# Router logits taken from the turned residual rows, with the norm factor, scale and shift applied to small tensors

## The reference

```python
sh1, sc1, g1, sh2, sc2, g2 = modulation(cond, mod_w, mod_b)
x = x + g1 * mixer(rms_norm(x, norm1) * (1 + sc1) + sh1)      # ends in: out = cat @ w_out
x = x + g2 * hierarchical_moe(rms_norm(x, norm2) * (1 + sc2) + sh2)
# in hierarchical_moe, xt = its input rows:
g_logits = xt @ rg_w + rg_b          # 4 groups: the best one
e_logits = xt @ re_w + re_b          # 32 experts: the best two of that group
y = grouped_expert_mlp(xt, expert_idx, weights, e_wg, e_wu, e_wd)
```

## Time and profile before

| | us |
|---|---|
| median of 3 runs | 1406.06 (1405.39 to 1408.11) |
| profiled execution | 1406.54 |
| its span in the trace | 1404.7 |
| busy in the span: PE, DVE, ACT, POOL | 1191.0, 706.3, 280.4, 107.9 |
| HBM traffic | 320.31 MB read, 25.51 MB written |

### The profile page before, as it was taken

How to read it: one execution, slowest core, us unless ns; L and a number is a source line. 1 busy time by engine, 2 the same in 40 slices (tenths; PEclk the granted TensorE clock), 3 DMA queues, 4 the chain that set the end, 5 groups by cost and what they waited for, 6 DMA issues and landing times.

```text
span 1404.7 us, 20219 instructions
## 1 busy us (share of the span) xinstructions
PE 1191.0 (85%) x7522; PEld 668.9 (48%) x7522; DVE 706.3 (50%) x1625; ACT 280.4 (20%) x700; POOL 107.9 (8%) x163
## 2 busy tenths in 40 slices
PE   5999999889787887897869999988979579699781
PEld 3455545654452544554434554556435354356450
DVE  3365877682467132232363687877634733223224
ACT  1211153750112000000032103356211100000000
POOL 2000000001000211111000000000100012012100
PEclk9999999999887898999989999999998779899896
DMA  9321101348149999999961101024561499999996
GB/s 376 150 94 47 54 21 60 129 172 338 77 166 381 407 421 418 419 419 419 397 247 53 71 33 58 1 75 175 220 276 72 180 348 417 419 419 419 419 413 249
DMA packets 59762, 334.58 MB, mean 238 GB/s; under 512 B 10672, under 2 KB 10672, under 8 KB 27404
## 3 DMA queue, kind: packets, MB, share of 16 engines
q1 hardware_dynamic: 45216, 295.78, 52.1%
q0 software_dynamic: 14448, 37.50, 7.1%
HBM read 320.31 MB, written 25.51 MB: 246 GB/s over the span
## 4 chain that ended last, share of the span: by engine, by line
PE 43%; DMA 21%; SPq 14%; DVE 10%; issue 5%; ACT 3%; DVEq 2%; PEld 1%; POOL 1%; PEldq 0%; ACTq 0%; POOLq 0%
PE bank L1762 12%; SPq L389 11%; DMA ring<-in_stream 11%; PE bank L1693 9%; DMA U<-in_stream 5%; PE bank L2061 4%; PE bank L2178 4%; DMA U<-in_n2row 3%; PE bank L2211 3%; SPq L387 2%; DVE U L1276 1%; PE bank L1637 1%; PE bank L1850 1%; DMA U<-moe_out 1%; PE bank L1876 1%
## 5 line engine op out<-in xcount | busy, mean ns | idle before, releaser
L1762 PE MATMUL bank<-HT,ring 128*128 128x512 f32 (+1 forms) x640 | 175.4, 435 | 2.0 <-issue 2.0
L2178 PE MATMUL bank<-ring,HT 128*32 128x256 f32 (+2 forms) x800 | 146.1, 433 | 33.7 <-DMA U<-in_stream 25.0
L2178 PE MATMUL bank<-U,HT 128*32 128x256 f32 (+2 forms) x992 | 151.7, 413 | 20.5 <-DMA ring<-in_stream 9.3
L1693 PE MATMUL bank<-ring,HT 128*128 128x512 f32 x320 | 147.1, 601 | 2.9 <-ACT HT L658 1.5
L1762 PEld LDWEIGHTS bank<-HT,ring 128*128 128x128 f32 x640 | 97.3, 191 | 79.7 <-issue 79.7
L2178 PEld LDWEIGHTS bank<-U,HT 128*32 128x32 f32 (+2 forms) x992 | 87.3, 136 | 59.5 <-issue 39.4
L1119 DVE SCALAR_TENSOR_TENSOR U<-U,prm 128x655 f32<-128x655 f32 x120 | 107.9, 899 | 7.7 <-issue 0.4
L2178 PEld LDWEIGHTS bank<-ring,HT 128*32 128x32 f32 (+2 forms) x800 | 80.2, 143 | 61.7 <-issue 46.3
L2061 PE MATMUL bank<-ring,HT 128*128 128x512 f32 x240 | 106.8, 594 | 0.0
L1555 DVE TENSOR_TENSOR HT<-bank,HT 128x256 f32<-128x256 f32 x32 | 13.6, 424 | 178.8 <-ACT HT L888 178.8
L888 ACT ACTIVATE HT<-bank 128x256 f32<-128x256 f32 x32 | 12.3, 384 | 412.8 <-PE bank L2178 412.8
(11 more groups left out here) (372 smaller groups left out, 1704.5 us busy)
## 6 DMA issues: line engine op xcount, KB each, us to landing
ring<-in_stream SPq DMA_DIRECT2D x142, 1024.0 KB, 14.1
U<-in_stream SPq DMA_DIRECT2D x72, 1024.0 KB, 25.6
spare<-in_stream SPq DMA_DIRECT2D x24, 1024.0 KB, 25.7
RAB<-in_stream SPq DMA_DIRECT2D x14, 1024.0 KB
U<-moe_out SPq DMA_DIRECT2D x20, 512.0 KB, 7.3
U<-in_stream SPq DMA_DIRECT2D x14, 512.0 KB, 20.4
CAT<-in_stream SPq DMA_DIRECT2D x14, 512.0 KB, 22.1
RAB<-mod_rows POOLq DMA_DIRECT2D x12, 512.0 KB, 9.3
```

The costliest lines, as they stand in the source:

```text
L1693: ins = e.matmul(bank[:], HT[:, k, t * P:(t + 1) * P], wide(q, k), start=(k == 0), stop=(k == KD - 1))
L1762: ins = e.matmul(out, wt(q)[:, k, P * (n % 2):P * (n % 2) + P], HT[:, k, lo:lo + w], start=(k == 0), stop=(k == KD - 1))
L2178: ins = e.matmul(PS[2 + p][s, FF * j:FF * j + FF], xgT[:, p, k, s], w, start=(k == 0), stop=(k == KD - 1))
```

## The change

The logits of a row x with norm factor r are r * (x @ (w * rw)) + (shift @ rw + rb), where w = norm weight * (1 + scale). The kernel after computes them in this form. `X` itself is turned (`x_turned`, `x_out` in place of `h2_turned`, `h2_out`), as soon as both halves of its residual are added. The scaled router weights are `rw0` for the context tile and `rw`, scaled in place, for the others. For the scale and shift as columns, PE multiplies the modulation rows in `srow` by two columns of the identity (`columns_of_rows`); the shift's logits are one row per condition (`shift_logits`), which DVE adds to `rb` and PE spreads over the partitions (`spread_shift`). `choice` applies r and adds the spread row, in one instruction per row tile. The normed rows `h2_row` are still made, for the experts. Orders, banks and the split of the choices (three tiles, then two) are changed with it. `residual(9)` stands behind the first choice. POOL waits for the columns before it loads `g1` over `srow`.

```diff
 # POOL, behind rows_out(l, 0, MODC)
+                e.wait_ge(S["shift_ps"], 4 * l + 2)
                 for cc in range(2):
                     e.dma_start(RA[:, cc, :], ...).then_inc(S["ld_g1"], 16)
 # ACT
                 for n in range(2 * NT):
                     if n in (2, 4):
                         cat_out(2 + n // 2)
+                    if 5 <= n < 9:
+                        x_out(n - 5)
                     e.wait_ge(S["x_added"], 10 * l + n + 1)
                     A(sqtmp, ..., ACT.Square, accum_out=small(1600 + n, 1))
...
-                    if n == 5:
-                        h2_out(0)
-                        h2_out(1)
-                for t in range(2, NT):
-                    h2_out(t)
+                x_out(NT - 1)
 # DVE
                 gated_rows(NT - 1, NT)
+                rw = pr("rw", KD, 36)
+                e.wait_ge(S["shift_ps"], 4 * l + 2)
+                e.scalar_tensor_tensor(out=rcol, in0=modcols[1]..., scalar=1.0, in1=pr("n2c")..., op0=ALU.add, op1=ALU.mult)
+                e.tensor_copy(bcol, modcols[0]).then_inc(S["shift_sb"], 1); dr()
+                e.tensor_tensor(rw0, rw, rcol[:, 0, :]..., ALU.mult)
                 cat_out(2)
                 e.wait_ge(S["ld_g1"], 32 * (l + 1))
...
                 residual(0)
                 residual(1)
                 cat_out(3)
+                residual(2)
+                residual(3)
+                cat_out(4)
+                residual(4)
+                e.wait_ge(S["shift_ps"], 4 * l + 3)
+                e.tensor_tensor(crow[0:2, :], crow_ps, pr("rb")[0:2, :], ALU.add).then_inc(S["shift_sb"], 1)
+                e.tensor_tensor(rw, rw, rcol[:, 1, :]..., ALU.mult)
+                residual(5)
+                e.wait_ge(S["shift_ps"], 4 * l + 4)
+                e.tensor_copy(cbias, cbias_ps)
+                e.drain().then_inc(S["shift_sb"], 1)
                 e.wait_ge(S["ld_rows"], 80 * (l + 1))
                 for cc in range(2):
                     e.scalar_tensor_tensor(out=RC[:, cc, :], ...)
-                for t in (0, 2):
-                    residual(2 * t + 2)
-                    residual(2 * t + 3)
-                    if t == 0:
-                        cat_out(4)
-                    y = norm2(t, 2, 1 + t // 2)
-                    h2_row(t, y[:, 0:1])
-                    residual(2 * t + 4)
-                    h2_row(t + 1, y[:, 1:2])
-                    residual(2 * t + 5)
-                h2_row(4, norm2(4, 1, 3))
+                norm2(0, 2, 1)
+                residual(6)
+                h2_row(0)
+                h2_row(1)
+                residual(7)
+                norm2(2, 2, 2)
+                h2_row(2)
+                residual(8)
+                h2_row(3)
...
-                    e.tensor_tensor(lg[:, t], logit_bank(t0)[:, 36 * t0:36 * t1]..., rb, ALU.add)
+                    for u in range(t0, t1):
+                        e.scalar_tensor_tensor(out=lg[:, u], in0=logit_bank(u)[:, 36 * u:36 * u + 36], scalar=small(1500 + u, 1),
+                                               in1=cbias[:, cnd(u), :], op0=ALU.mult, op1=ALU.add)
...
-                choice(0, NT - 1)
+                choice(0, LOGITS)                       # LOGITS = 3
+                residual(9)
+                norm2(4, 1, 3)
+                h2_row(4)
                 e.wait_ge(S["lg_ps"], 2 * l + 2)
-                choice(NT - 1, NT)
+                choice(LOGITS, NT)
 # PE
+                def x_turned(t):
+                    e.wait_ge(S["x_added"], 10 * l + 2 * t + 2)
+                    turned_tile(t, "xT_ps", ("x2T_a",), range(KD), X)
+                def columns_of_rows():
+                    e.wait_ge(S["fill_sb"], mod_chunks(l, 0) + MODC // 2)
+                    e.wait_ge(S["ct_sb_a"], NT * l + 2)
+                    e.wait_ge(S["ct_sb_d"], NT * l + 2)
+                    for i in range(2):
+                        r = slice(32 * i + 32, 32 * i + 34)
+                        for k in range(KD):
+                            ins = e.matmul(modcols[i][:, k, :], srow[r, k * P:(k + 1) * P], ident[r, 32 * i + 32:32 * i + 34], ...)
+                        ins.then_inc(S["shift_ps"], 1)
+                def shift_logits():
+                    for k in range(KD):
+                        ins = e.matmul(crow_ps, bcol[:, k, :], rw[:, k, :], start=(k == 0), stop=(k == KD - 1))
+                    ins.then_inc(S["shift_ps"], 1)
+                def spread_shift():
+                    e.wait_ge(S["shift_sb"], 3 * l + 2)
+                    for c in range(2):
+                        ins = e.matmul(cbias_ps[:, c, :], ident[0:2, c:c + 1].to_broadcast((2, P)), crow[0:2, :], ...)
+                    ins.then_inc(S["shift_ps"], 1)
...
                     projected(2 * t)
-                    cat_turned(t + 2)
+                    if t == 0:
+                        columns_of_rows()
+                    else:
+                        cat_turned(t + 2)
                     projected(2 * t + 1)
                     if t == 0:
-                        e.wait_ge(S["fill_sb"], mod_chunks(l, 0) + MODC // 2)
+                        e.wait_ge(S["shift_sb"], 3 * l + 1)
+                        cat_turned(2)
...
-                h2_turned(0)
+                shift_logits()
+                x_turned(0)
+                spread_shift()
                 projected(6)
-                h2_turned(1)
+                e.wait_ge(S["shift_sb"], 3 * l + 3)
+                x_turned(1)
+                projected(7)
                 logits(0)
+                x_turned(2)
+                projected(8)
                 logits(1)
-                for n in range(7, 10):
-                    projected(n)
-                h2_turned(2)
-                h2_turned(3)
+                x_turned(3)
                 logits(2)
+                projected(9)
                 logits(3)
-                h2_turned(4)
+                x_turned(4)
                 logits(4)
```

More of the change, by code:

```diff
@@ L250, in build @@
         sqtmp = view(INU * SLOT + 3 * D, 512)
+        rw0 = view(INU * SLOT + 3 * D + 512, KD, 36)
+        rcol = view(INU * SLOT + 3 * D + 512 + KD * 36, 2, KD)
+        bcol = view(INU * SLOT + 3 * D + 528 + KD * 36, KD, 2)
+        crow = view(INU * SLOT + 3 * D + 544 + KD * 36, 36)
+        cbias = view(INU * SLOT + 3 * D + 580 + KD * 36, 2, 36)
         colsum = PS[6][:, 0:32]
+        modcols = [PS[2 * i][:, 0:2 * KD].rearrange("p (k c) -> p k c", c=2) for i in range(2)]
+        crow_ps = PS[3][0:2, 64:100]
+        cbias_ps = PS[3][:, 128:200].rearrange("p (c n) -> p c n", c=2)
         frow = RAB[0:2].rearrange("p a b -> p (a b)")[:, D:4 * D]
@@ L2075, in logits @@
                         if k % 4 == 0:
-                            e.wait_ge(S["h2T_a"], 2 * (NT * l + t) + k // 4 + 1)
-                        ins = e.matmul(logit_bank(t)[:, 36 * t:36 * t + 36], HT[:, k, t * P:(t + 1) * P], rw[:, k, :], start=(k == 0), stop=(k == KD - 1))
-                    if t >= NT - 2:
+                            e.wait_ge(S["x2T_a"], 2 * (NT * l + t) + k // 4 + 1)
+                        ins = e.matmul(logit_bank(t)[:, 36 * t:36 * t + 36], HT[:, k, t * P:(t + 1) * P], (rw if t else rw0)[:, k, :],
+                                       start=(k == 0), stop=(k == KD - 1))
+                    if t in (LOGITS - 1, NT - 1):
                         ins.then_inc(S["lg_ps"], 1)
@@ L2098, in _, with before @@
-                h2_turned(2)
-                h2_turned(3)
+                x_turned(3)
                 logits(2)
+                projected(9)
                 logits(3)
-                h2_turned(4)
+                x_turned(4)
                 logits(4)
                 mods, q1 = MODBANK, b + INN + MODC + OUTN
-                e.wait_ge(S["wo_sb"], 10 * (l + 1))
+                ranks = PS[7][:, 0:NE * (NT + 1)].rearrange("p (t n) -> p t n", n=NE)
+                def before(j):
+                    return e.matmul(ranks[:, j + 1:, :], ones16[:].to_broadcast((P, P)), M16[:, j:j + 1, :].to_broadcast((P, NT - j, NE)),
+                                    start=(j == 0), stop=(j == NT - 1), skip_group_check=True)
@@ L2107, in _ @@
                 e.wait_ge(S["lg_sb"], 2 * l + 1)
-                e.matmul(PS[6][:, 0:NE], triS[:], M16[:, 0, :], start=True, stop=True, skip_group_check=True)
-                for j in range(NT - 1):
-                    e.matmul(PS[6][:, NE * (j + 1):NE * (NT + 1)].rearrange("p (t n) -> p t n", n=NE), ones16[:].to_broadcast((P, P)),
-                             M16[:, j:j + 1, :].to_broadcast((P, NT - j, NE)), start=(j == 0), stop=False, skip_group_check=True)
-                e.matmul(PS[6][:, NE:NE * (NT - 1)], triS[:], M16[:, 1:NT - 1, :], start=False, stop=False, skip_group_check=True)
+                e.matmul(ranks[:, 0, :], triS[:], M16[:, 0, :], start=True, stop=True, skip_group_check=True)
@@ L2113, in _ @@
+                for j in range(LOGITS):
+                    before(j)
```

(8 more changed lines are left out.)

47 lines of the change are left out of this document (25 added, 22 removed).

## The result

| | before | after |
|---|---|---|
| median of 4 runs, us | 1406.37 (1405.39 to 1408.11) | 1385.64 (1383.24 to 1387.75) |
| profiled execution, us | 1406.54 | 1387.75 |
| its span, us | 1404.7 | 1386.0 |

The ratio is 0.9851, 95% interval [0.9828, 0.9873]: 20.7 us faster, where I had forecast 12 and a range down to 1386. The unchanged kernel after, run again on another chip, has 0.9848 [0.9821, 0.9875].

A forecast was written before the change was run, and what follows sets the result against it. It took the start of the full expert DMA stream, set by the PE and DVE chain, as the bound. Gains of 7.7 and 9.8 us, less 5.7 for the clock, took 11.8 off 1406.54, forecast 1394 us, range 1386 to 1403.

The forecast's parts named there:

- The bound: Both layers' expert rounds: DMA is full, so each us taken from what starts the stream is one us of time.
- Behind projection 9: Projection 9's end to the choices' end: 13.85 us in place of 19.9, 6.0 us less in each layer.
- PE up to projection 9: Projection 0's start to projection 9's end: PE never stops, 85.9 us; 1.7 and 3.8 us less than before.
- The clock: Light matmuls between projections can drop PE to half clock without idleness; three spells of 1.9 us, 5.7 us in all.
- the eight places: Four light PE places a layer between projections: columns, shift group, logits 0 with a turn, logits 1 and 2 with a turn.
- The rival without any spell: No cold spells on PE: 1406.1 - 17.5 = 1388.6 us; chance 0.22.
- The luck in the sum: Gains of 7.7 us in the first layer and 9.8 in the second, 17.5 us, less 5.7 for the clock: 11.8.
- The stall: PE idle 7.8 or 8.8 us ahead of projection 6 before, plus 3.8 and 4.9 us at half clock; after, none.
- The other engines: Ahead of projection 9: POOL's loads come 2 us later, rows land at about 356 us, with 6 us of cover.
- the margin of DVE: Behind projection 8: DVE has 10.5 us of work against PE's 11.4, about even, DVE just ahead.
- The rival of DVE's order: The first choice starts only when projection 9 ends, giving back 6.5 us a layer; about 1401 us, chance 0.12.
- The slower rival: Added light PE work, dearer columns and a cold spell behind each light place make it slower: 1411.8 us, chance 0.09.

The follow-up runs named there:

- before_split: Kernel before, old arithmetic, with tiles 0 and 1 chosen between residuals 6 and 7 and tiles 2 to 4 at the end; 1416.99 us, ratio 1.0083.
- choice_late: Kernel after with the first choice moved behind residual 9, norm2(4) and h2_row(4), so all choices lie behind projection 9; 1398.23 us, ratio 0.9955.
- cols_x2: Kernel after with each of the 16 column matmuls issued twice, the same values written again; 1399.80 us, ratio 0.9966.
- stall_back: Kernel after, but PE waits ahead of projection 6 until the first normed row tile is made, ahead of residual 6; 1410.57 us, ratio 1.0040.
- before_split2: As before_split on the kernel before, with ranks of tiles 0 and 1 and chunk 0 issued without waiting for the second choice; 1407.24 us, ratio 1.0011.
- rows_early: Kernel after, but DVE waits for the five row loads and builds RC behind cat_out(3), ahead of residual 2; 1391.27 us, ratio 0.9908.
- cols_wide: Kernel after with 32 moving columns in place of 2 in each of the 16 column matmuls; 1384.72 us, ratio 0.9859.
- pool_row4: Kernel after with tile 4's normed row taken off DVE: ACT multiplies by the norm factor, GpSimd does the rest; 1391.48 us, ratio 0.9905.

## Why the prediction was wrong

- **The bound.** Right. The choices' end to the first layer's last scatter took 279.3 to 280.4 us in thirteen of the fourteen traces, with choices that ended anywhere from 411.20 to 428.56 (`before_split`, whose ranks came late behind chunk 0, has 283.9); none of the moved time was lost in the stream.
- **Behind projection 9.** Right: 13.85 us forecast, 14.1 and 13.8 measured; 6 us a layer forecast, 5.8 and 6.1 measured. `choice_late` gave the first choice back at 6.3 and 6.7 us.
- **PE up to projection 9.** The sum at full clock was 85.9 us, measured 85.1 where no spell fell and no new wait was made. The columns took 3.24 us (3.7 forecast). The shift's logits took 0.61 us, not 1.8: I had priced them as router logits, which have 128 columns of weights and took 0.107 us an instruction, while these have 2 and took 0.038. `shift_logits` is the term of the sum that was too dear, 1.2 us a layer. With both terms as measured the sum would be 84.2, so it misses 0.9 us elsewhere.
- **The clock: the step that failed.** "I take three spells in the eight places, 3 * 1.9 = 5.7 us." The mechanism exists: `cols_x2` shows a busy PE falling to half clock in light work. But only the columns' place ever had one, about every other time. The other three places (shift group, logits 0 with a turn, logits 1 and 2 with a turn, up to 4.8 us) had none in any of the eleven traces with the new arithmetic, apart from the half clock behind the wait that `stall_back` put in. I had carried the second layer's logits pair of before over to them. That pair stood one projection behind an idle PE, and so does the pair in every layer of the old arithmetic: `before`, `before_split` and `before_split2` had a spell behind it in three of six. That the idleness ahead is what makes the difference is likely, not shown. Rows 6 were weak evidence too: PE had waited 4.21, 0.60 and 0.39 us in the 11 us ahead of L1657 (timeline of PE of the kernel before). A spell was also priced too high: 3.8 us at a clock of 0.55 cost 1.7 us, not 1.9. One spell in place of three is 1.7 us in place of 5.7. The rival without any spell, 1388.6 by my sum, was the better forecast, and I had given it 0.22.
- **The luck in the sum.** With these two terms put right it is 17.5 + 2.4 - 1.7 = 18.2 us, and the profiled executions differ by 18.8. That they agree so well is luck: the changed stretches give 17.2 (the columns were 0.5 us a layer cheaper than in the sum, and it misses 0.9), and 2.0 of the 18.8 is the mixer, which had fewer spells in the execution of after (clock 0.96 against 0.94).
- **Outside the range.** The median's 20.7 us has an interval of 17.9 to 24.2. By the changed stretches alone, 17.2 us, it would have been 1389, inside the range; the further 3.5 us are not shown in any trace. The mixer's scatter of 6.7 us between executions is large enough for them. That scatter I had not looked for; it should have widened the range downwards as well.
- **The stall.** I had 3.8 and 4.9 us "at half clock" as what was left over of a sum. In the trace of before PEclk is 0.50 from 366.06 to 371.60 and from 1053.20 to 1057.70, which costs 2.8 and 2.2 us, and the second layer's spell 1.7 more; the last 1.0 us of each is not in the sum at all. `stall_back` measured 11.8 and 11.6 us for 9.0 and 8.7 of idleness.
- **The other engines.** POOL's `g1` load began at 326.06, forecast 325.5, against 323.49; in the kernel after nobody waited for the rows. Asked for early they landed at 357.15 (`rows_early`), against 353.81 before. The first choice ended at 401.47 and residual 9 started at 401.97: the margin of DVE was 0.5 us, forecast as about even. The rival of DVE's order is out for this kernel, though it is near.
- **The slower rival** needed 8.7 us a layer of extra light work. `cols_x2` came near it, with 5.1 and 8.5 us, and was still 0.34% faster than before.

## What to carry to other kernels

When a long step of one engine covers the wait for another's data, as the choice of four tiles did here, moving that step may gain nothing by itself: find the algebra that lets the data start earlier (here a factor that commutes with the matmul), then move the step under what is left. Price a PE stall at its idle time plus the cold spell behind it (here 11.8 us for 9.0). Compare the clock of unchanged stretches between traces before a difference of a few us is put down to an edit. Before forecasting cold spells from one occurrence in a trace, look at what stood ahead of it, and give the case without them its full weight.

## What the runs showed of the hardware

- TensorE fell from 2.4 to 1.2 GHz inside back-to-back matmuls with two rows of weights and two moving columns, busy 3.40 of 3.40 us (`cols_x2`). With 32 moving columns it could fall as well (`cols_wide`). The Trainium skill (TensorE: Matmul & The Clock Gate, "What's actually happening") gives the cold state to an engine that has been idle; these rows do not agree with that, since PE had no gap.
- An instruction with 36 moving columns (an f32 matmul is two such) took 0.038 us with 2 columns of weights (0.61 / 16) and 0.107 us with 128 (1.71 / 16, logits 0 in the chain of the kernel after).
- A DVE tensor_tensor that overlapped a GpSimd tensor_tensor of 128x1024 f32 lasted until about when that ended, 2.09 and 2.29 us in place of 0.17 and 0.23. A DVE tensor_reduce, which has one input, took its usual 0.16 us at 407.00, when GpSimd's had begun at 406.95 (`pool_row4`).
- The same 1001 matmuls of the mixer took PE 121.4 us at a granted clock of 1.00 and 127.9 at 0.94, with 14.1 and 13.4 us of idle time between them (`cols_x2`, before).
